# Attention's products of the 16 meta keys with V: one float32r product of 96 stacked rows in place of float32 products of 16 rows

## The chip, the cores and the metric

One core of one Trainium2 chip runs the whole program. The metric is the device time of one execution in microseconds (us); the median of a few executions counts. A difference of 0.2% (about 5.4 us) is what a measurement of this kernel can tell from no change.

## The reference, cut to what matters

The program computes two transformer blocks on a sequence of 1024 tokens. The change touches the first one only, which has two layers, 1024 features and 16 learned meta tokens ahead of the sequence, so 1040 positions. In each layer attention is done twice, once by four "differential" heads and once by eight "forgetting" heads:

```python
s = einsum('bhmqd,bhmkd->bhmqk', qb, k) * scale       # differential: two maps per head
p = softmax(where(visible, s, -inf), axis=-1)
a = p[:, :, 0] - lam * p[:, :, 1]
out = einsum('bhqk,bhkd->bhqd', a, v)                 # v is 128 wide

s = einsum('bhqd,bhkd->bhqk', qb, k) * scale + cq[..., None] - cum_logf[:, :, None, :]
p = softmax(where(visible, s, -inf), axis=-1)         # forgetting
out = einsum('bhqk,bhkd->bhqd', p, v)                 # v is 64 wide
```

The rows that matter here are the keys k of the last product: 1024 keys of the sequence, in 8 tiles of 128, and the 16 meta keys, which every query sees.

## The kernel before, in words

**Groups, blocks and maps.** The heads are worked in eight groups g. Groups 0 to 3 are one differential head each (its two softmax maps are merged on VectorE before the product with V, so there is one product map, 128 columns of V wide). Groups 4 to 7 are two forgetting heads each (two product maps m, 64 columns wide each, that write to the two halves of PSUM's partitions). Queries are worked in blocks of two tiles of 128, `BLOCKS` = (6,7), (4,5), (2,3), (0,1), and in layer 0 a last block (8,) of the 16 meta queries alone; layer 1 leaves that one out, since its output is not needed.

**Steps of a block.** `step_scores` computes the scores (float32r products on 64 rows) into PSUM, `step_max`, `step_exp` and `step_norm` make the softmax in tile `P` (part of `top`). Then `step_tr` transposes P with TensorE, two key tiles at a time, into one of three PSUM banks (`FEW` = 5, 6, 7); the first part (n = 0) is the 16 meta keys alone, "tile 8". `step_pt` copies each part to `PT` (also part of `top`), on ScalarE (L1894) or VectorE (L2657, and L2659/L2660 for the last, half empty part), as the planner chose. When all parts are copied, `step_av` multiplies with V: for each key tile one float32 product per map. Tile 8 comes first: `V[0:16]` against `PT[0:16]`, 16 rows, 256 query columns. A tile that only the second query tile sees has 128 columns. `step_av_out` (L1856) takes the result out of PSUM.

**How V gets there.** `step_turn_v` transposes the projected V in three pieces (quads); quad 2 is the 16 meta rows, and `step_v_out` on ScalarE copies them into `V[0:16, ..., 8, :]` (L1869).

**Precision.** A product of float32 tiles appears in the trace as two weight loads and two MATMUL records. A product of float32r tiles has one of each. Where the kernel uses float32r it splits each operand into a high part (a float32r copy) and a low part (the rest), and makes three products: high x high, high x low, low x high. The projections (`step_unit`, `mm3`) do this: `AH`, `AL` are the activations, `WH`, `WL` the weights.

**What sets the order.** `attention_order` plans each layer before the program is built: `Clocks` keeps a model of when TensorE, ScalarE, VectorE, GpSimd and the DMA queue are free, and puts the next TensorE step from four lists (scores; transposes and products with V; projection units of the next groups; small ones), and the evacuations by `PRIORITY` and due time. The cost of a step stands in `cost` and `side_of`: a product step costs 216 ns for the last tile, 432 for each other, 610 for tile 8, plus 150. Projection units fill the time between attention steps, one at a time in one of the three `FEW` banks. Each engine then runs its list in that order.

All helper calls record the same source line: L1078 is every product, L1087 every transpose, so steps are told apart by the tiles they read. `PS<-top,V` are the products with V, `PS<-AH,WH` and so on the projection units, `PS<-ident,top` the transposes of P, `PS<-KH,QH` and `PS<-maskr,eyer` the scores.

## Time and profile before

| what | value |
|---|---|
| median of 3 runs | 2723.8 us (2722.2 to 2727.41) |
| the profiled execution's own time | 2731.44 us |
| its span, first to last instruction | 2729.6 us |
| mean granted TensorE clock | 0.988 |
| TensorE busy (MATMUL) | 2649.7 us, 97% |
| VectorE / ScalarE / GpSimd busy | 1637.5 / 1201.0 / 466.2 us |
| layer 0's attention, layer 1's attention | about 100 to 720 us, about 840 to 1500 us |

The profiled execution is 1.8 us longer than its span and 7.6 us longer than the median. A row of the timeline gives the start and the length of an instruction (or of a run of like ones); on TensorE the lengths overlap, since a product's record begins when it is taken up and ends when its last result is out, so cost is read from start to start. PE is TensorE's products, PEld its weight loads, DVE VectorE, ACT ScalarE. Shapes read as rows*columns of the stationary operand, then rows x columns of the moving one.

### The profile page before, as it was taken

What the parts mean: (1) busy time and instruction counts of PE and PEld (TensorE: products, weight loads), DVE (VectorE), ACT (ScalarE), POOL (GpSimd) and SP (SyncE); (2) the same over time, 40 slices, a digit from 0 to 9 for tenths busy, and PEclk for the clock granted to TensorE, in tenths of its full rate; (3) what the DMA queues carried; (4) which work ended last, traced back from release to release, by engine and by line L of the source; (5) the groups of instructions that cost most, each with busy time, mean ns of one, the idle gap of its engine ahead of it and who ended that gap; (6) DMA issues with size and microseconds to landing.
All of it is one profiled execution on the core that took longest, in us unless ns stands there. A gap on an engine that the chain in (4) does not pass through costs nothing.

```text
span 2729.6 us, 43070 instructions
## 1 busy us (share of the span) xinstructions
PE 2649.7 (97%) x16632; PEld 2278.5 (83%) x16632; DVE 1637.5 (60%) x2944; ACT 1201.0 (44%) x2372; POOL 466.2 (17%) x674
## 2 busy tenths in 40 slices
PE   6999999999999999999999999999998999999999
PEld 6888888888899888878777997888897788887887
DVE  5766664444535666554446366555437877778767
ACT  6444444333424444443334462223335655555444
POOL 2211232310001222452000124000013101011000
PEclk9999999999999999999999899999998999999999
DMA  4121377761312212897202423113232344444443
GB/s 150 57 67 64 120 191 198 202 158 44 142 58 74 74 64 74 245 233 182 82 24 78 129 72 114 47 47 100 93 92 95 116 127 121 124 126 153 177 154 135
DMA packets 219225, 314.21 MB, mean 115 GB/s; under 512 B 15478, under 2 KB 157494, under 8 KB 219022
## 3 DMA queue, kind: packets, MB, share of 16 engines
q0 software_dynamic: 50304, 151.30, 19.2%
q1 hardware_dynamic: 168720, 160.16, 18.6%
q8 instruction: 134, 2.20, 0.3%
q14 instruction: 67, 0.55, 0.1%
HBM read 267.26 MB, written 111.22 MB: 139 GB/s over the span
## 4 chain that ended last, share of the span: by engine, by line
PE 84%; DVE 6%; ACT 3%; issue 2%; DMA 2%; POOL 2%; SPq 0%; DVEq 0%; ACTq 0%; POOLq 0%
PE PS L1078 79%; PE PS L1087 5%; DMA T<-TMP 2%; DVE WL L2451 1%; DVE AL L2494 1%; POOL TMP L3427 1%; DVE ST L2623 0%; DMA R<-s_adap 0%; DVE TMP L2606 0%; POOL T L3424 0%; DVE T L2599 0%; ACT top L1881 0%; ACT TMP L1830 0%; DVE top L2636 0%; ACT TMP L1720 0%
## 5 line engine op out<-in xcount | busy, mean ns | idle before, releaser
L1078 PE MATMUL PS<-AH,WH 128*128 128x344 f32 (+2 forms) x2160 | 805.0, 373 | 23.7 <-DVE AL L2494 9.4
L1078 PE MATMUL PS<-AL,WH 128*128 128x344 f32 (+2 forms) x2160 | 756.8, 350 | 0.0
L1078 PE MATMUL PS<-AH,WL 128*128 128x344 f32 (+2 forms) x2160 | 756.3, 350 | 0.0
L1078 PEld LDWEIGHTS PS<-AH,WH 128*128 128x128 f32 x2160 | 408.8, 189 | 83.5 <-issue 21.0
L1078 PEld LDWEIGHTS PS<-AH,WL 128*128 128x128 f32 x2160 | 408.5, 189 | 36.0
L1078 PEld LDWEIGHTS PS<-AL,WH 128*128 128x128 f32 x2160 | 409.8, 190 | 32.1 <-issue 1.0
L1078 PE MATMUL PS<-WH,AH 128*128 128x256 f32 (+1 forms) x972 | 309.4, 318 | 3.7 <-DVE WL L2451 3.7
L1078 PE MATMUL PS<-WL,AH 128*128 128x256 f32 (+1 forms) x972 | 308.6, 317 | 0.0
L1078 PE MATMUL PS<-WH,AL 128*128 128x256 f32 (+1 forms) x972 | 308.6, 317 | 0.0
L2623 DVE TENSOR_REDUCE ST<-PS 128x1 f32<-128x784 f32 (+8 forms) x272 | 187.9, 732 | 143.0 <-PE PS L1078 142.5
L2451 DVE TENSOR_TENSOR WL<-W,WH 128x1024 fp32r<-128x1024 f32 x157 | 192.6, 1229 | 125.6 <-ACT WH L1708 125.5
L1881 ACT ACTIVATE top<-PS,ST 128x784 f32<-128x784 f32 (+8 forms) x272 | 194.9, 722 | 111.7 <-DVE ST L2623 87.7
L1708 ACT ACTIVATE WH<-W 128x1024 fp32r<-128x1024 f32 x157 | 165.3, 1055 | 119.9 <-PE PS L1078 105.4
L1078 PEld LDWEIGHTS PS<-WH,AH 128*128 128x128 f32 x972 | 185.5, 191 | 18.6 <-issue 4.5
L1078 PEld LDWEIGHTS PS<-WH,AL 128*128 128x128 f32 x972 | 185.6, 191 | 12.1
L1078 PEld LDWEIGHTS PS<-WL,AH 128*128 128x128 f32 x972 | 185.5, 191 | 12.0
L1078 PE MATMUL PS<-top,V 128*64 128x256 f32 (+6 forms) x1176 | 183.3, 373 | 2.9 <-DVE top L2660 2.4
L1087 PE MATMUL PS<-ident,top 128*128 128x128 f32 (+2 forms) x1132 | 172.5, 276 | 5.9 <-DVE AL L2494 3.3
L1078 PEld LDWEIGHTS PS<-top,V 128*64 128x64 f32 (+3 forms) x1176 | 119.6, 154 | 67.3 <-issue 39.3
L1087 PEld LDWEIGHTS PS<-ident,top 128*128 128x128 f32 (+2 forms) x1132 | 127.7, 133 | 32.6 <-ACT top L1894 3.8
L1894 ACT ACTIVATE top<-PS 128x512 f32<-128x512 f32 (+1 forms) x167 | 82.7, 500 | 147.3 <-PE PS L1087 146.0
L3147 DVE TENSOR_TENSOR WL<-W,WH 128x512 fp32r<-128x512 f32 x116 | 90.3, 781 | 75.1 <-ACT WH L2230 75.1
(406 smaller groups left out, 4419.5 us busy)
## 6 DMA issues: line engine op xcount, KB each, us to landing
W<-in_k_w_in SPq DMA_DIRECT2D x66, 512.0 KB, 4.2
s_wt<-in_w_up POOLq DMA_DIRECT2D x96, 352.0 KB, 6.3
W<-in_w_ada SPq DMA_DIRECT2D x48, 512.0 KB, 5.2
s_wd<-in_w_down POOLq DMA_DIRECT2D x66, 256.0 KB, 6.3
W<-s_wt SPq DMA_DIRECT2D x64, 256.0 KB, 3.5
W<-in_w_in SPq DMA_DIRECT2D x28, 512.0 KB, 3.8
W<-in_w_up SPq DMA_DIRECT2D x52, 256.0 KB, 3.3
W<-in_w_out SPq DMA_DIRECT2D x24, 512.0 KB, 3.5
```

Of the source, the lines that this page charges most:

```text
L1078: return e.matmul(out, lhsT, rhs, start=start, stop=stop, skip_group_check=True)
L1087: return e.transpose(out, in_, ident[0:k, 0:k])
L1708: e.activation(high(v), W32[:, s, :], ACT.Copy).then_inc(*w_hi.mark(v))
L1881: e.activation(P[0:rows, P_SLOT[u], 0:W], PSf[0:rows, o:o + W], ACT.Exp, bias=st[:, 0:1], accum_out=st[:, 1:2]).then_inc(*exped.mark(u))
L1894: e.activation(o, i, ACT.Copy).then_inc(*pt_act.mark(key))
L2451: e.tensor_tensor(low(v), W32[:, slot32(v), :], f(high(v)), ALU.subtract).then_inc(*w_lo.mark(v))
L2494: e.scalar_tensor_tensor(lo, bank(b)[:, o:o + n], COLS[:, 8 * l + k:8 * l + k + 1], f(hi), ALU.mult, ALU.subtract).then_inc(*fill_lo.mark( ...
L2623: e.tensor_reduce(ST[0:rows, ST_SLOT[u], 0:1], PSf[0:rows, o:o + W], AX.X, ALU.max, negate=True).then_inc(*row_max.mark(u))
L3147: e.tensor_tensor(lo, up_source(i), f(hi), ALU.subtract).then_inc(*w_lo.mark(("up", i)))
L3427: e.tensor_tensor(TMP[:, cc:cc + nn], TMP[:, cc:cc + nn], cosT[:, cc:cc + nn], ALU.mult).then_inc(*rope_cos.mark(key))
```

## The change

The meta keys' product becomes float32r on 96 rows. Rows 0 to 31 of the stacked P hold the high part of the transposed probabilities, rows 32 to 63 the low part, rows 64 to 95 the high part again; the stacked V holds high, high, low. One product so sums the three terms. Only 16 of each 32 rows are real; the transposes now turn 32 columns, and the surplus rows of V are multiplied by 0 (a new constant column, `OF_META`).

- New tiles `V3a`, `V3b` (stacked V, one for each parity of the group) and `P3` (stacked P, two slots); `V` and `PT` lose their ninth tile.
- For two-map groups each map's product is 128 columns wide, the other map's 64 columns of V3 being zero, so both maps add into the whole bank, one after the other.
- `step_pt` makes two copies instead of one for part 0, on the same engine. A new VectorE step `pt_lo` makes the low part and only then frees the bank. `step_v_out` for quad 2 makes two copies (four for two-map groups), and a new VectorE step `v_lo` makes V's low part.
- `step_av` waits for `v_lo` and `pt_lo` beside the other parts; the product of tile 8 stays the first.
- The planner's costs follow (tile 8 costs 210 instead of 610; the meta block 200 instead of 400; part 0's copies 600 or 750 ns, `pt_lo` 440, `v_lo` 500), so the whole order of both layers is planned anew.

```diff
-            V = own("V", [128, 2, 9, 128])[:, :, :, :]
+            V, V3a = own("V", [128, 2, 8, 128])[:, :, :, :], own("V3a", [128, 256], F32R)
...
-            top = own("top", [128, 4 * L + 2 * 9 * 256])
+            top = own("top", [128, 4 * L + 2 * 8 * 256])
+            P3 = own("P3", [128, 2, 256], F32R)
+            V3 = [V3a[:, :], own("V3b", [128, 256], F32R)[:, :]]
...
                     if blk == (8,):
-                        return 400
+                        return 200
...
-                    return sum(216 if t == blk[1] else 432 if t < 8 else 610 for t in tiles) + 150
+                    return sum(216 if t == blk[1] else 432 if t < 8 else 210 for t in tiles) + 150
...
-                b = turn_bank(("pt",) + key, (pt_act if PT_SIDE[key] == "act" else pt_dve, key))
+                b = turn_bank(("pt",) + key, (pt_lo if n == 0 else pt_act if PT_SIDE[key] == "act" else pt_dve, key))
...
+                        if t == 8:
+                            x = tr(e, bank(b)[0:32, 128 * jj:128 * jj + rows], P[0:rows, P_SLOT[l, g, j, m], 0:32])
...
-                e.wait_ge(*v_turned.at((l, g, 2)))
+                e.wait_ge(*v_turned.at((l, g, 1)))
+                e.wait_ge(*v_lo.at(("v", l, g)))
                 for m in maps(g):
-                    for n in range(len(parts(l, g, bi))):
+                    e.wait_ge(*pt_lo.at((l, g, bi, m, 0)))
+                    for n in range(1, len(parts(l, g, bi))):
...
-                        kr = NM if t == 8 else 128
-                        qa = 128 if (not meta and t == blk[1]) else 0
-                        x = mm(e, bank(b)[r0:r0 + rn, qa:nq], V[0:kr, vs, t, r0:r0 + rn], PT[0:kr, PT_SLOT[l, g, bi, m], t, qa:nq],
-                               i == 0, i == len(tiles) - 1)
+                        if t == 8:
+                            x = mm(e, bank(b)[:, 0:nq], V3[vs][0:96, 128 * m:128 * m + 128], P3[0:96, slot_, 0:nq], m == 0, meta and m == maps(g)[-1])
+                        else:
+                            qa = 128 if t == blk[1] else 0
+                            x = mm(e, bank(b)[r0:r0 + rn, qa:nq], V[:, vs, t, r0:r0 + rn], PT[:, slot_, t, qa:nq], False, i == len(tiles) - 1)
...
+                    if n == 0:
+                        e.activation(P3[64:96, PT_SLOT[l, g, bi, m], 0:i.shape[1]], i, ACT.Copy)
                     e.activation(o, i, ACT.Copy).then_inc(*pt_act.mark(key))
...
+                        if n == 0:
+                            e.tensor_copy(P3[64:96, pt, 0:i.shape[1]], i)
                         e.tensor_copy(o, i).then_inc(*pt_dve.mark(key))
...
+                def step_pt_lo(g, bi, m, n):
+                    key = (l, g, bi, m, n)
+                    pt, nq, b = PT_SLOT[l, g, bi, m], NM if BLOCKS[l][bi] == (8,) else 256, banks.place.get(("pt",) + key, 0)
+                    side_ = pt_act if PT_SIDE[key] == "act" else pt_dve
+                    e.wait_ge(*side_.at(key))
+                    e.tensor_tensor(P3[32:64, pt, 0:nq], bank(b)[0:32, 0:nq], f(P3[0:32, pt, 0:nq]), ALU.subtract).then_inc(*pt_lo.mark(key))
+
+                def step_v_lo(g):
+                    vs, b = g % 2, banks.place.get(("vt", l, g, 2), 0)
+                    e.wait_ge(*v_turned.at((l, g, 2)))
+                    if g in (4, 5):
+                        e.tensor_tensor(V3[vs][0:96, 64:192], ident[0:96, :], ident[0:96, :], ALU.subtract)
+                    for (o, i), (hi, _) in zip(cols3(g, vs, 64, 96, b), cols3(g, vs, 0, 32, b)):
+                        x = e.scalar_tensor_tensor(o, i, OF_META[0:32, :], f(hi), ALU.mult, ALU.subtract)
+                    x.then_inc(*v_lo.mark(("v", l, g)))
```

## Rows read from the trace of the kernel before

**Rows 1.** The page's part 1: TensorE's busy time, share of the span, instructions

```profile
PE 2649.7 (97%) x16632; PEld 2278.5 (83%) x16632; DVE 1637.5 (60%) x2944; ACT 1201.0 (44%) x2372; POOL 466.2 (17%) x674
```

**Rows 2.** The page's part 4: the chain that ended last, by engine

```profile
PE 84%; DVE 6%; ACT 3%; issue 2%; DMA 2%; POOL 2%; SPq 0%; DVEq 0%; ACTq 0%; POOLq 0%
```

**Rows 3.** Busy times in both layers' attention; last columns: PEclk, DMA share, GB/s

```profile
100.00:720.00 620.00, 610.53 (x4489) 527.76 (x4486) 353.29 (x785) 261.53 (x586) 130.31 (x192) 1.00 0.43 121
840.00:1500.00 660.00, 647.34 (x4418) 538.22 (x4417) 377.46 (x761) 284.04 (x578) 149.02 (x221) 0.99 0.40 112
```

**Rows 4.** PE's longest waits, 100 to 720 and 840 to 1500: total, times, longest

```profile
PE PS L1078 <- ACT FIN L1901: 3.3, 2, 1.7
...
PE PS L1078 <- ACT top L1881: 4.6, 7, 2.0
```

**Rows 5.** PE's timeline around two product steps of one-map groups: start, length

```profile
114.88 4.13 PE L1078 MATMUL PS<-top,V 16*128 16x256 f32 x18
118.77 0.40 PE L1078 MATMUL PS<-AH,WH 128*128 128x344 f32 x1
...
138.03 0.32 PE L1078 MATMUL PS<-AH,WL 128*128 128x344 f32 x1
138.28 3.27 PE L1078 MATMUL PS<-top,V 16*128 16x256 f32 x14
141.30 0.40 PE L1078 MATMUL PS<-AH,WH 128*128 128x344 f32 x1
141.54 0.31 PE L1078 MATMUL PS<-AL,WH 128*128 128x344 f32 x1
```

**Rows 6.** The weight loads of the second of these steps, idle time in brackets

```profile
138.27 0.29 PEld L1078 LDWEIGHTS PS<-top,V 16*128 16x128 f32 x2 [0.22 <-issue]
138.90 2.46 PEld L1078 LDWEIGHTS PS<-top,V 128*128 128x128 f32 x12 [0.33 <-issue]
141.27 0.19 PEld L1078 LDWEIGHTS PS<-AH,WH 128*128 128x128 f32 x1
```

**Rows 7.** PE's timeline around a product step of a two-map group

```profile
430.22 0.31 PE L1078 MATMUL PS<-AH,WL 128*128 128x344 f32 x1
430.47 4.04 PE L1078 MATMUL PS<-top,V 16*64 16x256 f32 x36
...
434.69 0.32 PE L1078 MATMUL PS<-AL,WH 128*128 128x344 f32 x1
```

**Rows 8.** The weight loads of that step

```profile
430.46 0.19 PEld L1078 LDWEIGHTS PS<-top,V 16*64 16x64 f32 x4 [0.21 <-issue]
431.04 3.22 PEld L1078 LDWEIGHTS PS<-top,V 128*64 128x64 f32 x32 [0.38 <-issue]
434.43 0.19 PEld L1078 LDWEIGHTS PS<-AH,WH 128*128 128x128 f32 x1 [0.17 <-issue]
```

**Rows 9.** PE's timeline in the output projection: float32r products of 256 columns

```profile
1499.92 0.28 PE L1078 MATMUL PS<-WH,AL 128*128 128x256 f32 x1
1500.04 0.28 PE L1078 MATMUL PS<-WH,AH 128*128 128x256 f32 x1
```

**Rows 10.** PE's timeline around a product step of the 16 meta queries

```profile
185.25 0.32 PE L1078 MATMUL PS<-AH,WL 128*128 128x344 f32 x1
...
185.82 0.39 PE L1087 MATMUL PS<-ident,top 128*16 128x128 f32 x2
```

**Rows 11.** Groups by shape, first 1500 us: evacuations; busy us, mean ns

```profile
L1894 ACT ACTIVATE top<-PS 16x256 f32<-16x256 f32 x59 | 21.9, 371 | 58.5 <-PE PS L1087 57.9
...
L2657 DVE COPY top<-PS 16x256 f32<-16x256 f32 x37 | 15.2, 410 | 9.7 <-PE PS L1087 9.2
...
L2590 DVE SCALAR_TENSOR_TENSOR KL<-PS,KH 128x344 fp32r<-128x344 f32 x16 | 8.1, 508 | 9.9 <-ACT KH L1834 9.9
```

**Rows 12.** The end of layer 0's attention, timeline

```profile
716.28 0.42 DVE L2659 COPY top<-PS 128x256 f32<-128x256 f32 x1 [0.38 <-PE PS L1087]
...
717.04 1.45 PE L1078 MATMUL PS<-top,V 16*64 16x256 f32 x12 [0.81 <-DVE top L2660]
```

More of the change, by code:

```diff
@@ L497, in build @@
         class Clocks:
-            PRIORITY = {"leave": 0, "leave_lo": 0, "pt": 0, "max": 1, "av_out": 0, "v_out": 0, "rope": 0, "rope_sin": 0, "ada_out": 1, "fin_ms": 1, "exp": 1, "norm": 1,
+            PRIORITY = {"leave": 0, "leave_lo": 0, "pt": 0, "max": 1, "av_out": 0, "v_out": 0, "pt_lo": 0, "v_lo": 0, "rope": 0, "rope_sin": 0, "ada_out": 1, "fin_ms": 1, "exp": 1, "norm": 1,
                         "forget": 2, "rope_add": 2, "rope_end": 2, "rope_lo": 2, "fin1": 2, "fin3": 2, "gate": 2, "split": 3, "split_lo": 3, "root": 3,
@@ L650, in place @@
                     out.append(("pt",) + st[1:])
+                    if n == 0:
+                        out.append(("pt_lo",) + st[1:])
                 elif what == "av":
@@ L663, in place @@
                         if st[2] == 2:
+                            out.append(("v_lo", st[1]))
                             self.tmp = [end] * 3
@@ L702, in side_of @@
                         return ready, 740
+                    if n == 0:
+                        return ready, (600, 750)
                     return ready, (170 + 1.02 * wide, 250 + 0.68 * wide)
+                if what == "pt_lo":
+                    return at["hi", st[1:]], 440
+                if what == "v_lo":
+                    return at["hi", "v", st[1]], 500
                 if what == "av_out":
@@ L788, in put_side @@
                     self.side[st[1:]] = engine
+                    if st[4] == 0:
+                        at["hi", st[1:]] = seen
+                    else:
+                        self.leave(("tr",) + st[1:], back)
+                        at[st] = back
+                elif what == "pt_lo":
                     self.leave(("tr",) + st[1:], back)
-                    at[st] = back
+                    at[("pt",) + st[1:]] = back
                 elif what == "av_out":
@@ L808, in put_side @@
                         at["qk", st[1], st[2]] = back
+                elif what == "v_out" and st[2] == 2:
+                    at["hi", "v", st[1]] = seen
                 elif what == "v_out":
@@ L811, in put_side @@
                     at[("v",) + st[1:]] = back
+                elif what == "v_lo":
+                    self.leave(("turn_v", st[1], 2), back)
+                    at["v", st[1], 2] = back
                 elif what == "ada_out":
@@ L1063, in build @@
         g_out, g_in = o_in, tile_in
+        pt_lo, v_lo = conv_v, g_v
         down_mm, down_act, down_dve, end_sq, end_v, out_done = (count("down_mm"), count("down_act"), count("down_dve"), count("end_sq"),
@@ L1187, in step_turn_v @@
                 key = (l, g, quad)
-                b = turn_bank(("vt",) + key, (v_turned, key))
+                b = turn_bank(("vt",) + key, (v_turned, key) if quad < 2 else (v_lo, ("v", l, g)))
                 e.wait_ge(*proj_out.at((l, g, "v", 2)))
-                for i, t in enumerate(range(4 * quad, min(4 * quad + 4, 9))):
-                    cc, n = (NM + 128 * t, 128) if t < 8 else (0, NM)
-                    m = tr(e, bank(b)[0:n, 128 * i:128 * i + 128], TMP[:, cc:cc + n])
+                if quad == 2:
+                    m = tr(e, bank(b)[0:32, 0:128], TMP[:, 0:32])
+                else:
+                    for i, t in enumerate(range(4 * quad, 4 * quad + 4)):
+                        m = tr(e, bank(b)[:, 128 * i:128 * i + 128], TMP[:, NM + 128 * t:NM + 128 * t + 128])
                 m.then_inc(*vt_mm.mark(key))
@@ L1260, in step_tr @@
                         e.wait_ge(*normed.at((l, g, j, 1 if g < 4 else m)))
-                kr = NM if part[0] == 8 else 128
                 for i, t in enumerate(part):
                     for jj, j in enumerate(blk):
-                        if t < 8 and t > j:
-                            continue
                         rows = NM if j == 8 else 128
-                        ka = 0 if t == 8 else NM + 128 * t
-                        x = tr(e, bank(b)[0:kr, 256 * i + 128 * jj:256 * i + 128 * jj + rows], P[0:rows, P_SLOT[l, g, j, m], ka:ka + kr])
+                        if t == 8:
+                            x = tr(e, bank(b)[0:32, 128 * jj:128 * jj + rows], P[0:rows, P_SLOT[l, g, j, m], 0:32])
+                        elif t <= j:
+                            ka = NM + 128 * t
+                            x = tr(e, bank(b)[:, 256 * i + 128 * jj:256 * i + 128 * jj + 128], P[:, P_SLOT[l, g, j, m], ka:ka + 128])
                 x.then_inc(*pt_mm.mark(key))
@@ L1868, in step_v_out @@
                     else:
-                        e.activation(V[0:NM, vs, 8, :], bank(b)[0:NM, 0:128], ACT.Copy).then_inc(*v_turned.mark((l, g, quad)))
+                        for o, i in cols3(g, vs, 0, 32, b):
+                            e.activation(o, i, ACT.Copy, scale=OF_META[0:32, :])
+                        for o, i in cols3(g, vs, 32, 64, b):
+                            x = e.activation(o, i, ACT.Copy, scale=OF_META[0:32, :])
+                        x.then_inc(*v_turned.mark((l, g, quad)))
                 def step_exp(g, j):
@@ L2425, in scalar, with cols3 @@
             ffn()
+        def cols3(g, vs, r0, r1, b):
+            if g < 4:
+                return [(V3[vs][r0:r1, 0:128], bank(b)[0:32, 0:128])]
+            return [(V3[vs][r0:r1, 192 * m:192 * m + 64], bank(b)[0:32, 64 * m:64 * m + 64]) for m in range(2)]
         def pt_evac(l, g, bi, part, pt, b):
@@ L2431, in pt_evac @@
                 nq = NM if blk == (8,) else 256
-                return PT[0:NM, pt, 8, 0:nq], bank(b)[0:NM, 0:nq]
+                return P3[0:32, pt, 0:nq], bank(b)[0:32, 0:nq]
             return PT[:, pt, part[0]:part[0] + 2, :].rearrange("p a b -> p (a b)"), bank(b)
@@ L3758, in layout @@
         cols[r:128:32, 20 + r % 2] = 1.0
+    for r in range(NM):
+        cols[r:128:32, 22] = 1.0
     a["k_cols"] = cols
```

9 lines of the change are left out of this document (7 added, 2 removed).

## The prediction, made before the changed kernel ran

> **What bounds the kernel now.** I read the busy shares first: TensorE is busy 97% of the span, VectorE 60%, ScalarE 44% [rows 1]. The chain that ended last is 84% TensorE [rows 2]. The change touches only the two layers' attention, so I asked for the busy times there: TensorE 610.5 of 620 us and 647.3 of 660 us, idle 9.5 and 12.7 us in all; VectorE 353 and 377 us (57%), ScalarE 262 and 284 us (43%) [rows 3]. The longest of TensorE's waits sums to 3.3 us in one layer and 4.6 us in the other [rows 4]. So TensorE bounds both stretches, and projection units fill the gaps between attention's steps. A microsecond taken from its products should shorten the span by nearly one, as long as the others keep up.
>
> **TensorE, one-map groups.** A product step of 18 records takes 3.89 us from its start to the next unit's, one of 14 records 3.02 us [rows 5]: four records more for 0.87 us, 0.216 us a record of 256 columns, 0.432 us a float32 product, half of that for 128 columns. From the last unit record before the second step (138.03) to the second one after it (141.54) are 3.51 us. Two units of 0.16 us belong to that, so the step costs 3.19 us. Its six tile products take 5 x 0.432 + 0.216 = 2.37 us. **Tile 8 so costs 0.82 us**, not 0.43. The other 0.39 us stand in the weight loads: the 16-row load begins only after 0.22 us of idle loader, the first 128-row load after 0.33 us, but the load of the unit behind the step has no idle time before it [rows 6]. A load of the same shape as the running product is hidden under it. Where the shape changes, it waits for the stream's end and is then exposed itself: some 0.195 us at each of the two changes.
>
> After the change tile 8 is one float32r product of 256 columns: 1500.04 - 1499.92 = 0.12 us [rows 9]. Its 96 rows are my first unknown; no row shows 96. If the array takes them as it takes 128, both changes of shape vanish and the step saves 0.82 - 0.12 = 0.70 us. If 96 counts as a shape of its own, both stay, and it saves 0.82 - 0.12 - 0.39 = 0.31 us. I take the first: 96 rows need more than half of the array, and a product of 128 rows is the nearest. There are 32 such steps (four groups, four blocks, two layers). 11 of them follow a score or a small product in the trace, where the entry stays exposed (0.51 us saved); 21 follow a unit. Sum: 21 x 0.70 + 11 x 0.51 = 20.3 us.
>
> **Two-map groups.** The two maps' products run side by side on 64 columns each: 36 records in the time of 18 [rows 7]. From 430.22 to 434.69 are 4.47 us, less two units 4.15, less 7 x 0.432 + 0.216 = 3.24 leaves 0.91 us. Of this 0.20 us is the way out to a unit: 0.17 us of idle loader, then an exposed load [rows 8]. That way out is not touched. Tile 8 so costs 0.71 us for the pair: 0.43 and two changes of shape of 0.14 each (the loads are half as wide). After: two products, one after the other because each covers all 128 columns, 2 x 0.12 = 0.24 us; the entry from a unit has no change of shape, but the change from 128 columns to 64 behind it stays, 0.14. Saved 0.71 - 0.24 - 0.14 = 0.33 us. This change of shape is where a rule speaks against the edit. The Trainium skill, TensorEngine Tiling (Array Packing), Key Properties, says that a change of tiling mode, not merely of the tile, drains TensorE; by that rule the trace's 0.14 us stay, and without a drain 32 x 0.14 = 4.5 us more would be saved. With 96 as its own shape the entry costs 0.195 and only 0.14 us are saved. Of 32 steps 27 follow a unit, 5 a score or a transpose (0.14 us): 27 x 0.33 + 5 x 0.14 = 9.6 us.
>
> **The eight steps of the meta queries**, layer 0 only. Now 185.82 - 185.25 - 0.16 = 0.41 us [rows 10]; one load of 128 columns in its place is about 0.12. I take 0.25 us each, between nothing and 0.41: 2 us.
>
> **Transposes.** The part of the meta keys turns 32 columns for 16, against the same 128 moving columns. Only their weight loads grow by 16 columns. If all of that were exposed, at the 0.195 us that an exposed 128-column load and its wait cost, it would be 0.195 / 8 on 108 parts, 2.6 us; I take nothing, since loads that follow a product of the same shape are hidden [rows 6].
>
> TensorE's sum: 20.3 + 9.6 + 2 = **32 us**; 15 us if 96 is its own shape (32 x 0.31 + 32 x 0.14 + 0.5).
>
> **VectorE and ScalarE.** There are 96 parts of meta keys of 256 columns and 12 of 16. Now each costs one copy, 371 ns on ScalarE (59) or 410 ns on VectorE (37) [rows 11]. The second copy adds 59 x 0.37 = 22 us and 37 x 0.41 = 15 us. `pt_lo` reads PSUM and a tile: the nearest row is 508 ns for 344 columns [rows 11], bounds for 256 columns are 0.41 (a copy's row) and 0.51; I take 0.42: 40 us, and 2 for the small ones. V's stacked rows, 16 groups of a few short pieces at 0.2 to 0.3: 7 us on VectorE, 7 on ScalarE. VectorE gains 64 us on 731, ScalarE 29 on 546, over 1250 us: 64% and 46% busy. That lies under TensorE's units while there are any. If the cover is gone, a meta part costs 0.41 + 0.42 + 0.06 us of signals more than now before its product may start.
>
> **Where it is not covered: the ends of the layers.** At the end of layer 0 no unit is left, and TensorE waits 0.81 us for VectorE's copies [rows 12]. Here the bank's two extra operations stand ahead of those copies in VectorE's queue. The last two blocks of layer 0 and of layer 1 pay; between nothing (ScalarE takes the copies) and 4 x 0.9 x 2 maps = 7 us. I take 3 us. In the middle, VectorE's wait for ScalarE's copy in `pt_lo` holds up the maxima and normalizations queued behind it, for which `step_exp` and `step_tr` wait, and a bank of the three is held some 0.9 us longer. Bounds: nothing, and as much idle time again as both stretches have now, 22 us [rows 3]. I take 3 us, as VectorE is a third idle even then.
>
> **Sum.** 32 - 3 - 3 = 26 us off the profiled execution's 2731.4 us. This one is 7.6 us above the median, 2723.8 us, so the median becomes **2698 us**. Own range of this case: 2690 (all 32 us and a luckier plan) to 2706.
>
> **Rivals.**
> 1. *96 rows is a shape of its own, or one of the drains stays.* TensorE then gains 15 us, less 6: 9 us, 2715 us. For it: all rows with a row count other than 128 pay (16 here) [rows 6]. Against: 16 rows use an eighth of the array, 96 cannot be packed beside anything. The Trainium skill's page named above lists row tilings of 128, 64 and 32 rows alone under Tiling Modes; it has none of 96, so by it this rival does not happen, and no row here shows it. Chance 0.13.
> 2. *The gain is half eaten by the side engines*: VectorE gets 64 us more and TensorE 32 us less cover; stalls of 16 us instead of 6 leave 16 us, 2708 us. For it: the three banks, and 4.6 us of waits on ScalarE's exponentials already [rows 4]. Against: a total idle time of 22 us in 1280 [rows 3]. Chance 0.09.
> 3. *The low part becomes the wait that sets the pace.* Every product step starts with tile 8, so it waits for `pt_lo` first. If `pt_lo` stands so late in VectorE's queue that TensorE idles 0.5 us or more in each of the 64 steps, the whole 32 us are gone; from there it is slower. At 0.8 us, what it waits at the layer's end today [rows 12], it loses 64 x 0.8 - 32 = 19 us: 2743 us. Against: part 0 is transposed first, and up to four more parts follow it, so it has more than a microsecond of lead in the long blocks. Only block (0,1) has a single part behind it. Chance 0.04.
> 4. *It doesn't do what it says*: the float32r product runs no faster than the float32 one. Then only the drains go and two-map groups get slower (two products for a pair side by side): 32 x 0.39 - 32 x (0.43 - 0.14) = 3 us less, 6 more lost: 2727 us. The float32r units speak against it [rows 9]. Chance 0.02.
>
> The likeliest case keeps 0.72. The range goes from 2690 to 2715, up to rival 1's figure; about 0.17 lie outside. Faster by over 0.2% (5.4 us, about what a measurement can tell) are the first case and rivals 1 and 2 but for their edges: 0.91. Within it 0.05, slower 0.04.
>
> **What the changed profile would show.** Tile 8's loads should read 96*128, and in one-map steps neither they nor the first 128*128 load behind them should have idle time before them (against 0.22 and 0.33 us [rows 6]); the step of the 14 records should shrink to 13 and by 0.7 us. In two-map steps an idle loader should remain ahead of the first 128*64 load. TensorE's busy time in the two stretches should fall by about 30 us, VectorE's rise by 64. Idle TensorE should grow by 6 us, mostly at the ends. I am wrong if the 96-row load stands after an idle gap (rival 1), if waits on `P3` or banks sum to over 15 us (rival 2), or if they come in every step (rival 3).

## The result, and the profile after

The changed kernel takes 2748.75 us (median of 4 runs, 2747.44 to 2750.02) against 2724.65 us for the kernel before beside it: a ratio of 1.0088, interval 1.0071 to 1.0106. It is 24 us slower where 26 us faster were forecast, and outside the range. The profiled execution took 2747.65 us, its span is 2745.9 us.

The page of the changed kernel, its busy times and its chain:

```profile
PE 2631.7 (96%) x16524; PEld 2283.4 (83%) x16524; DVE 1702.8 (62%) x3132; ACT 1227.4 (45%) x2460; POOL 466.5 (17%) x674
...
PE 77%; DVE 8%; issue 7%; ACT 4%; DMA 2%; POOL 2%; ACTq 0%; DVEq 0%; SPq 0%; POOLq 0%
```

TensorE has 18 us less to do than in [rows 1]; VectorE has 65 us more and ScalarE 26 us more, close to what was foreseen. But TensorE's share of the chain fell from 84% [rows 2] to 77%. Busy times in the two stretches of [rows 3] (last columns PEclk, DMA share, GB/s):

```profile
100.00:720.00 620.00, 595.38 (x4395) 527.81 (x4392) 371.07 (x853) 273.85 (x631) 129.96 (x191) 0.99 0.43 121
840.00:1500.00 660.00, 636.97 (x4334) 541.69 (x4334) 403.58 (x828) 284.29 (x590) 150.80 (x222) 0.99 0.40 113
```

TensorE's busy time fell by 25.5 us, 30 were foreseen (VectorE's rose by 44 us in these two stretches; the rest of its 65 us lies outside them). But the work did not go forward: both stretches hold 178 records fewer than before (4395 + 4334 against 4489 + 4418), some 100 of them the change's own, and the rest were done later. The time saved went idle.

**The product steps did shrink.** TensorE's products and weight loads around the one-map step of [rows 5 and 6], now with 13 records in place of 14:

```profile
139.24 0.33 PE L1102 MATMUL PS<-AH,WL 128*128 128x344 f32 x1
139.41 0.28 PE L1102 MATMUL PS<-P,V3a 96*128 96x256 f32 x1
139.53 2.54 PE L1102 MATMUL PS<-top,V 128*128 128x256 f32 x12
141.83 0.40 PE L1102 MATMUL PS<-AH,WH 128*128 128x344 f32 x1
142.07 0.32 PE L1102 MATMUL PS<-AL,WH 128*128 128x344 f32 x1
```

```profile
139.25 0.19 PEld L1102 LDWEIGHTS PS<-P,V3a 96*128 96x128 f32 x1
139.41 2.47 PEld L1102 LDWEIGHTS PS<-top,V 128*128 128x128 f32 x12
141.80 0.19 PEld L1102 LDWEIGHTS PS<-AH,WH 128*128 128x128 f32 x1
```

No idle loader is left before either load, and from the last unit record before the step to the second one after it are 142.07 - 139.24 = 2.83 us, against 3.51: 0.68 us saved, 0.70 were foreseen. So 96 rows run as 128 do. The two-map step of [rows 7 and 8] has now:

```profile
430.29 0.30 PEld L1102 LDWEIGHTS PS<-P,V3a 96*128 96x128 f32 x2 [0.32 <-DVE GT L2628]
430.73 3.22 PEld L1102 LDWEIGHTS PS<-top,V 128*64 128x64 f32 x32
434.12 0.19 PEld L1102 LDWEIGHTS PS<-AH,WH 128*128 128x128 f32 x1 [0.17 <-issue]
```

Tile 8 takes 430.73 - 430.29 = 0.44 us of the loader for the pair, against 431.04 - 430.46 = 0.58 [rows 8]; the step is 3.83 us long instead of 3.97. This step stands behind a wait. In the 24 two-map steps that follow a projection unit directly the pair takes 0.34 us (median from the first record to the next tile's), before 0.58. Added up from start to start over all product steps, idle gaps left out, they fell from 173.5 to 149.4 us, and the records just ahead of them, which bear the entry, from 18.1 to 14.3 us: 28 us saved. Of these, 19.5 us lie in the one-map steps, 7.0 in the two-map steps and 1.2 in those of the meta queries.

In the two-map step 0.14 us lie between the end of the second load, at 430.59, and the next one; in 30 of the 32 two-map steps this gap is 0.13 or 0.14 us. The Trainium skill, TensorEngine Tiling (Array Packing), Key Properties, has a change of tiling mode drain TensorE; the trace agrees with it.

**Where it went.** Added up in the same way, TensorE's idle gaps from 60 us to the output projection in layer 0, and from 850 us in layer 1, were 13.3 + 10.4 = 23.7 us before and are 32.6 + 28.2 = 60.7 us now. TensorE's waits in the whole program (total, times, longest):

```profile
PE PS L1102 <- ACT top L1915: 12.0, 20, 2.0
PE PS L1102 <- DVE P L2711: 10.5, 9, 2.3
...
PE PS L1111 <- DVE P L2711: 5.2, 9, 1.4
...
PE PS L1111 <- ACT OTt L1886: 4.1, 2, 3.1
PE PS L1102 <- ACT OTt L1886: 3.9, 3, 3.0
PE PS L1102 <- DVE V3a L2719: 3.6, 3, 1.3
```

L2711 is `pt_lo`: products wait for it 10.5 us, transposes for the bank that it holds 5.2 us. L1915 is the exponentials, for which TensorE waited 6.4 us in the whole program before:

```profile
PE PS L1078 <- ACT top L1881: 6.4, 10, 2.0
```

L1886 is `step_av_out`; before, TensorE waited 0.4 us in all for it. The cause of the new wait can be read in three views, ScalarE's and TensorE's timelines, and the busy times from 430 us:

```profile
428.81 0.46 ACT L1853 ACTIVATE GT<-PS 128x344 f32<-128x344 f32 x1 [0.63 <-PE PS L1102]
442.23 0.38 ACT L1886 ACTIVATE OTt<-PS 128x256 f32<-128x256 f32 x1 [12.97 <-DMA s_os<-OTt]
```

```profile
442.67 0.41 PE L1111 MATMUL PS<-ident,top 128*32 128x128 f32 x2 [3.06 <-ACT OTt L1886]
445.30 1.12 PE L1111 MATMUL PS<-ident,top 128*128 128x128 f32 x4 [2.22 <-DVE GT L2628]
```

```profile
430.00:440.00 10.00, 9.41 (x70) 7.71 (x67) 1.49 (x3) 0.00 (x0) 1.94 (x3) 1.00 1.05 238
440.00:450.00 10.00, 5.11 (x23) 4.67 (x23) 2.89 (x5) 2.87 (x5) 0.00 (x0) 0.66 0.06 26
```

The next group's result may not be written to `OTt` until the gate's store `s_os<-OTt` of the group before has landed. GpSimd issues that store at 429.98 us, behind a burst of eight background transfers (last two rows of the burst, and the store):

```profile
428.94 1.60 POOL L3455 DMA_DIRECT2D s_wt<-s_wt  x1
429.46 1.91 POOL L3458 DMA_DIRECT2D s_wt<-s_wt  x1
429.98 1.95 POOL L3491 DMA_DIRECT2D s_os<-OTt  x1
```

It lands 12.2 us later. ScalarE does nothing from 430 to 440 us, then TensorE runs dry twice. From 442.9 to 449.7 us, so from the end of the first gap on, its granted clock is the lower one: 0.66 on average from 440 to 450 us, its units starting every 0.29 us at the lower of the two levels (1.2 GHz) in place of 0.16 us at 2.4. From 100 us to the end of layer 1's attention, the stretches at the lower level add up to 37.5 us, before to 13.7 us. TensorE was idle in 5.2 us of the 37.5 and in 0.3 us of the 13.7. Half of what is left is lost: 16 us now, 7 us before, so 9 us more.

The sum over the two layers is then 28 us saved, 37 us more idle, 9 us more by the clock, and some 3 us in the transposes of 32 columns: 21 us longer. The traces agree: the output projection of layer 1 starts at 1520.0 us instead of 1499.6, 20.4 us later. This is not the whole of the 24 us between the medians. The two profiled executions are only 16 us apart, since the one of before was 7 us above its median, and behind that point the changed kernel's execution is 4 us the faster one, though nothing was changed there. So the parts of the sum are good to a few microseconds, not to one.

### The profile page after: what moved, and what is told of

Same layout as the page of the kernel before. It is cut to its first block, busy times and chain, and to the rows that moved or that the text cites. A ratio compares the mean times of both kernels' runs of the same rounds, so it can differ in the third digit from the quotient of the medians.

```text
span 2745.9 us, 43150 instructions
## 1 busy us (share of the span) xinstructions
PE 2631.7 (96%) x16524; PEld 2283.4 (83%) x16524; DVE 1702.8 (62%) x3132; ACT 1227.4 (45%) x2460; POOL 466.5 (17%) x674
## 4 chain that ended last, share of the span: by engine, by line
PE 77%; DVE 8%; issue 7%; ACT 4%; DMA 2%; POOL 2%; ACTq 0%; DVEq 0%; SPq 0%; POOLq 0%
PE PS L1102 72%; PE PS L1111 4%; DMA T<-TMP 1%; DMA s_os<-OTt 1%; DVE ST L2665 1%; ACT top L1915 1%; DVE AL L2536 1%; DVE WL L2493 1%; DVE P L2711 0%; POOL TMP L3487 0%; DVE top L2681 0%; DVE P L2701 0%; ACT R L1983 0%; DVE top L2701 0%; ACT TMP L1860 0%
## 5 line engine op out<-in xcount | busy, mean ns | idle before, releaser
L1915 ACT ACTIVATE top<-PS,ST 128x784 f32<-128x784 f32 (+8 forms) x272 | 194.5, 721 | 93.0 <-DVE ST L2665 68.6
L1102 PE MATMUL PS<-top,V 128*64 128x256 f32 (+1 forms) x960 | 139.8, 368 | 0.0
L1102 PEld LDWEIGHTS PS<-top,V 128*64 128x64 f32 (+1 forms) x960 | 102.8, 157 | 30.9 <-issue 2.3
L3469 POOL DMA_DIRECT2D s_adap<-AST x48 | 29.1, 606 | 532.5 <-DVE AST L2573 515.9
```

Of the source, the lines that this page charges most:

```text
L1102: return e.matmul(out, lhsT, rhs, start=start, stop=stop, skip_group_check=True)
L1915: e.activation(P[0:rows, P_SLOT[u], 0:W], PSf[0:rows, o:o + W], ACT.Exp, bias=st[:, 0:1], accum_out=st[:, 1:2]).then_inc(*exped.mark(u))
L3469: e.dma_start(adap[i % 2][:, 256 * (i // 2):256 * (i // 2) + 256], AST[:, i % 2, :]).then_inc(*ada_out[i % 2].landed(i))
```

## Experiments

Idle is TensorE's, added up as above in each profile. The ratio compares the means of the runs with the runs of the kernel before that were taken beside them. Their medians lay between 2724.65 and 2727.25 us, so kernels are best compared by the ratio, and 0.001 of it is 2.7 us. In a row of idle times 2 us mean nothing: the gap of 1.5 to 2.3 us with which layer 1 begins falls ahead of 850 us in some kernels and behind it in others.

| kernel | operations | order planned by | us | ratio to before (interval) | idle us |
|---|---|---|---|---|---|
| before | old | before | 2724.65 | 1 | 23.7 |
| after | new | after | 2748.75 | 1.0088 (1.0071 to 1.0106) | 60.7 |
| oldops_newplan | old | after | 2747.69 | 1.0082 (1.0064 to 1.0100) | 40.8 |
| newops_oldplan | new | before | 2765.14 | 1.0141 (1.0120 to 1.0162) | 70.8 |
| nolo | new, no `pt_lo` | after | 2735.43 | 1.0033 (1.0022 to 1.0045) | 51.8 |
| nolo_oldplan | new, no `pt_lo` | before | 2715.90 | 0.9965 (0.9953 to 0.9976) | 38.5 |
| oldops_loplan | old | low parts alone | 2777.72 | 1.0188 (1.0170 to 1.0207) | 62.2 |
| newops_loplan | new | low parts alone | 2778.70 | 1.0187 (1.0170 to 1.0203) | 81.6 |
| store_first | new, sums later | after | 2740.99 | 1.0051 (1.0037 to 1.0064) | 53.6 |
| late | new, tile 8 last | after | 2744.05 | 1.0066 (1.0052 to 1.0080) | 60.3 |
| both | both of these | after | 2737.88 | 1.0047 (1.0034 to 1.0060) | 53.2 |
| onecopy | new, one copy less | after | 2739.12 | 1.0047 (1.0031 to 1.0063) | 56.1 |
| truecost | new | after, copies at 860 | 2751.41 | 1.0093 (1.0079 to 1.0106) | 67.5 |
| oldplan_late | new, tile 8 last | before | 2759.76 | 1.0120 (1.0104 to 1.0136) | 71.0 |
| before620 | old | before, tile 8 at 620 | 2724.17 | 0.9997 (0.9986 to 1.0007) | 23.2 |
| k128 | float32, 128 rows | before | 2714.44 | 0.9959 (0.9946 to 0.9972) | 26.5 |
| k128_store | same, sums later | before | 2713.22 | 0.9957 (0.9944 to 0.9969) | 29.1 |
| k128_432 | same | before, tile 8 at 432 | 2720.43 | 0.9978 (0.9968 to 0.9987) | 31.8 |

**Operations against order.** oldops_newplan is the kernel before with the changed planner (`Clocks` and `attention_order`); the new steps that it plans are not issued.

> The products, copies and waits of the kernel before, but every engine's list in the order that the changed planner makes (its costs, with pt_lo and v_lo planned and then not issued). Theory A, the new order carries the loss (background transfers, banks and queues meet otherwise): 15 to 35 us slower than before, 2740 to 2760 us. Theory B, the low part's own operations and waits carry it: within 6 us of before, 2719 to 2731 us. In between means both.

newops_oldplan is the changed kernel with the planner of before, each low part put right behind its copy:

```diff
+        def with_low(steps):
+            out = []
+            for st in steps:
+                out.append(st)
+                if st[0] == "pt" and st[4] == 0:
+                    out.append(("pt_lo",) + st[1:])
+                if st[0] == "v_out" and st[2] == 2:
+                    out.append(("v_lo", st[1]))
+            return out
```

> The changed operations, but every engine's list in the order of the planner of before, pt_lo put directly behind its copy and v_lo behind V's copy. Theory A: the saving on TensorE (24 us from start to start in the two traces) shows, less a few us of stalls: 2702 to 2714 us. Theory B: the stalls come again: 2735 to 2755 us.

The old operations lose 22 us (1.0082) in the new order: theory A held, and the order alone is as slow as the whole change. But the new operations lose more in the old one, 38 us, which is slower than either theory allowed. There, VectorE's queue stands at `pt_lo` for ScalarE's copy (VectorE's waits, in that kernel and in the changed one):

```profile
DVE P L2703 <- ACT P L1922: 65.5, 41, 6.0
```

```profile
DVE P L2711 <- ACT P L1930: 8.4, 24, 0.6
```

The changed planner brings these 65.5 us down to 8.4: it makes the room that the low part needs, and pays with an order that is worse in other places. For the new operations as a whole the new order is the better one, by 14 us (1.0141 less 1.0088). A part of the 38 us may belong to the placing in this run, which puts each low part directly behind its copy, also where the copy is ScalarE's; a low part that stands later in VectorE's queue was not run in the old order.

The two runs split the result. In the new order the new operations take 2 us more than the old ones (1.0088 less 1.0082), though they save 28 us on TensorE: what they bring with them costs 30 us there, the transposes' 3 us among it. So the 24 us are 22 us of order and 30 us of the operations' own stalls, less 28 us saved. In the old order these stalls cost 66 us (38 and the 28 saved).

**Without the low part.** nolo is the changed kernel in its own order without `pt_lo`:

```diff
-                    e.wait_ge(*pt_lo.at((l, g, bi, m, 0)))
-                    for n in range(1, len(parts(l, g, bi))):
+                    for n in range(len(parts(l, g, bi))):
...
                 def step_pt_lo(g, bi, m, n):
-                    key = (l, g, bi, m, n)
...
+                    return
```

> The changed kernel in its own order, but pt_lo is not issued: rows 32 to 63 of P3 stay zero, the bank is free after the copy and the product waits for the copy only. It leaves out the term P low x V high. All other operations and their order are the same. Theory A: the order's stalls stay, 2738 to 2748 us. Theory B: the 16 us of TensorE's waits on pt_lo and what hangs on them go, 2715 to 2730 us.

nolo took 2735 us, between the two outcomes: 15 us come back (1.0088 less 1.0033), and part of the stalls stays. nolo_oldplan is the same in the order of before.

> The new operations in the order of the kernel before, without the low part of P's meta rows (that part of the product is left out: P low with V high), so with the second copy and V's low part alone as extra work. The same without the low part in the changed order took 2735 us. If the changed order itself costs some 20 us whatever the operations (as it does for the old ones), this one runs at 2735 - 20 = 2715 us or under; TensorE's 24 us saved less the second copies' stalls would then at last be seen below the kernel before. If the changed order is only bad for operations that don't have the low part, it is no faster than 2735 us. With the low part in this order 2765 us were measured; so the difference to it is what the low part costs where the order makes no room for it: 30 to 50 us by the first theory.

The first theory held: 2715.9 us, 9.5 us faster than before, and 19.5 us faster than in the new order. So the new order costs 22 us with the old operations and 18 us without the low part (1.0033 less 0.9965), and the low part costs 15 us in the new order (1.0088 less 1.0033) and 48 us in the old one (1.0141 less 0.9965). Even without either, of the 28 us saved on TensorE 18 are gone, to the second copies, V's low part and the longer chain: 38.5 us idle against 23.7.

**A third order.** oldops_loplan and newops_loplan take the changed planner with the old costs of TensorE's steps:

```diff
-                        return 200
+                        return 400
...
-                    return sum(216 if t == blk[1] else 432 if t < 8 else 210 for t in tiles) + 150
+                    return sum(216 if t == blk[1] else 432 if t < 8 else 610 for t in tiles) + 150
```

> The kernel before with its own operations, in the order that the changed planner gives when it plans the low parts but keeps the old costs of TensorE's product steps (610 for the meta tile, 400 for the meta queries). It splits the 23 us by which the old operations lose in the changed order (2748 us). If planning with TensorE's cheaper steps spoils the order (the planner thinks that VectorE and ScalarE are late and the background goes to other places), this one runs at about 2727 us. If the low parts' 440 and 600 ns in the side engines' queues spoil it, about 2747 us. If any change of order does about as much harm, between them, with other stores behind other transfers.

> All new operations, in the order of a planner that knows the low parts but keeps the old costs of TensorE's product steps. The old operations took 2778 us in this order, 30 us more than in that of the full planner. If a bad order is bad for any operations, this one takes about 2749 + 30 = 2779 us; if it was bad only because that planner expected slower side engines than the old operations have, it comes to about 2750 us.

Both take 51 us more than before, to within a microsecond of each other, so here too the stalls of the new operations eat the 28 us that they save. For the first run this was none of the three outcomes that I gave; for the second, the first outcome came. It is not a rule that an order is as bad for any operations: in the order of before the new ones lose 38 us. TensorE's longest wait of all in oldops_loplan, and in oldops_newplan, is for the exponentials, 6.4 us in the kernel before:

```profile
PE PS L1098 <- ACT top L1901: 26.1, 21, 3.7
```

```profile
PE PS L1098 <- ACT top L1901: 13.1, 18, 2.0
```

These operations are untouched by the change, and their wait goes with the order, whatever the operations: 6.4 to 9.0 us in the six kernels whose TensorE, ScalarE and VectorE follow the order of before, 11.3 to 13.4 in the seven that follow that of the changed kernel, 26 in both of this third order. That they come late since the scores, maxima and exponentials stand elsewhere in the queues is argued, not shown. The opposite planner, with the new TensorE costs alone, was not run.

**The stores.** In store_first GpSimd's background sums go behind a gate's store that follows directly:

```diff
                         if at_ > turns:
-                            weight_sums(next(sums))
+                            held = [x[0] for x in STEPS[l][at_ + 1:] if x[0] in ("ada_out", "rope", "gate", "reload")][:1] == ["gate"]
+                            if not held:
+                                weight_sums(next(sums))
```

> The changed kernel with one thing moved: on GpSimd's queue a group of background transfers (the weight sums, eight or more of them) that stands directly ahead of the store of a finished group is issued behind that store. In the new order three stores of layer 0 stand behind such a group (at 430, 503 and 591 us), in the order of before none stands behind more than four. If this collision carries the order's loss: ScalarE's longest wait for a store falls from 13 us to under 5 and the kernel is 8 to 15 us faster than the changed one, 2733 to 2741 us. If it only explains the one gap at 440 us: 2742 to 2746 us. If nothing: 2747 to 2751 us.

It takes 2741 us: some 8 to 10 us of the loss. ScalarE's longest wait for a store falls from 13.0 to 3.5 us. This wait belongs to the order and not to the operations, since the old ones have it too (ScalarE's waits in oldops_newplan and in the kernel before):

```profile
ACT OTt L1876 <- DMA s_os<-OTt: 24.5, 5, 14.0
```

```profile
ACT OTt L1856 <- DMA s_os<-OTt: 11.9, 6, 3.1
```

In store_first the stretch that had been empty is full again:

```profile
430.00:440.00 10.00, 10.00 (x73) 9.17 (x69) 3.48 (x7) 3.44 (x6) 0.76 (x1) 1.00 1.02 213
440.00:450.00 10.00, 9.78 (x80) 8.09 (x80) 6.24 (x19) 4.20 (x12) 6.12 (x9) 1.00 0.75 249
```

**Where the wait stands.** late takes tile 8 last in each product step, and waits for `v_lo` and `pt_lo` only there:

```diff
+                tiles = tiles[1:] + tiles[:1]
                 for i, t in enumerate(tiles):
+                    if t == 8:
+                        e.wait_ge(*v_lo.at(("v", l, g)))
+                        for m in maps(g):
+                            e.wait_ge(*pt_lo.at((l, g, bi, m, 0)))
```

> The changed kernel in its own order, but the product of the meta keys stands last in its step and the waits on pt_lo and v_lo stand directly before it. If the low part costs by making the product wait (10.5 us of waits on P before products): 2738 to 2744 us. If it costs by holding one of three banks and by VectorE's time: unchanged, 2746 to 2751 us.

It gains some 5 us, but its interval (1.0052 to 1.0080) overlaps that of the changed kernel. The product comes later and still waits: products wait 8.8 us for `pt_lo`, without this edit 10.5, and the transposes' 5.2 us of waits for the bank stay (5.1). So the run moves the wait and hardly removes it. both joins it with store_first.

> Both partial remedies in the changed kernel: tile 8's product last with its waits (late, measured 2744 us) and GpSimd's background sums behind the gate's store (store_first, 2741 us), against 2749 us unmended. If the two losses are separate they add up: 2749 - 8 - 5 = 2736 us, 1.003 to 1.004 of before. If they are one loss seen twice (the late product only bridges the time in which ScalarE stands at the store) it stays at about 2741 us. If the idle time amplifies itself through the halved clock, the two together give more than their sum, under 2732 us.

2737.9 us lies between 2736 and 2741, with intervals that overlap those of store_first: the second remedy adds at most a few microseconds to the first, and the run doesn't settle how many. oldplan_late is late in the order of before.

> All new operations in the order of the kernel before (2765 us), with tile 8's product moved from first to last in each step and its waits with it. If those 2765 us come from the waits of the product steps on VectorE's P3 (10.2 us of waits there, and the clock that falls in them), late products take 10 to 20 us off: 2750 us. If they come from the bank held longer and from VectorE's own wait for ScalarE's copy (65.5 us over 41 waits in that order), which the maxima and normalizations queue behind, it stays at 2762 us or more.

It took 2760 us, between the two outcomes, and its interval overlaps that of newops_oldplan. Here too the waits did not go: products wait 11.1 us for `pt_lo` (10.4 in newops_oldplan), and VectorE waits 64.6 us for ScalarE's copy (65.5). So the run doesn't tell what these waits cost. That the low part as a whole costs 48 us in this order is shown by nolo_oldplan; how this divides between the products' waits, the held banks and VectorE's queue is not.

**Length or load.** onecopy leaves out the second copy (rows 64 to 95 of `P3` stay zero).

```diff
-                        if n == 0:
-                            e.tensor_copy(P3[64:96, pt, 0:i.shape[1]], i)
```

> The changed kernel, same order, without the second copy of P's high part (rows 64 to 95 of the stacked tile stay zero, so the product of P's high with V's low part is left out). 37 copies of about 0.43 us leave VectorE and 59 of 0.37 leave ScalarE. If it is the length of the chain between a transposed part and its product (copy, copy, low part) that makes the stalls, 0.4 us of 1.3 go from each of 108 chains and the time falls about as far as without the low part's subtraction (2735 us): 2737 us. If only VectorE's queue counts, 15 us less work there gives a third of what leaving out the low part gave (13.5 us for 47 us of VectorE's work): 2745 us. If the order alone counts: 2749 us, nothing.

11 us come back (1.0088 to 1.0047), nearly as much as without `pt_lo` (15 us), though VectorE loses 16 us of work here and 41 us there. TensorE's waits for `pt_lo` fall from 15.7 to 11.4 us. This speaks for the first theory, the length of the chain from a transposed part to its product, and against VectorE's load alone. It doesn't part the chain from ScalarE, which loses 21 us of work here and none in nolo, nor from the bank, which is free one copy earlier.

**Truer costs.** truecost plans the two copies closer to what they take on VectorE (415 and 413 ns, and what lies between); before620 plans the kernel before with 10 ns more for tile 8.

```diff
-                        return ready, (600, 750)
+                        return ready, (860, 750)
```

```diff
-                    return sum(216 if t == blk[1] else 432 if t < 8 else 610 for t in tiles) + 150
+                    return sum(216 if t == blk[1] else 432 if t < 8 else 620 for t in tiles) + 150
```

> The changed kernel, with the planner's cost of part 0's two copies on VectorE at the 860 ns that the trace shows (two starts 0.43 us apart and the next 0.45 us later) instead of 600. If stalls come from a plan that thinks VectorE faster than it is: 5 to 12 us faster than the changed kernel, 2736 to 2744 us. If not: another order with stalls like these, 2744 to 2755 us.

> The kernel before, where the planner's cost of tile 8 is 620 ns instead of 610. No operation changes, only the order. If the order of before is one that any small move of a cost spoils (a lottery in which before holds a good ticket): 5 us or more away from before, most likely slower, 2730 to 2745 us. If orders from nearly equal costs are equally good, and the new one is bad for its own reasons: within 4 us of before.

Neither moved the time beyond its interval. But before620 hardly moves the order either: of the 3835 steps in the planner's lists of both layers only some 40 stand elsewhere than in the kernel before, against some 300 between truecost and the changed kernel, and some 1700 between the changed kernel and the one before. So these two runs show that small moves do no harm. They don't show that a plan made wholly anew is no throw of dice.

**The change of shape alone.** k128 is the kernel before with tile 8's float32 product over 128 rows, the 112 that are no meta keys multiplied by zero:

```diff
-                        kr = NM if t == 8 else 128
+                        kr = 128
...
-                        e.activation(V[0:NM, vs, 8, :], bank(b)[0:NM, 0:128], ACT.Copy).then_inc(*v_turned.mark((l, g, quad)))
+                        e.activation(V[:, vs, 8, :], bank(b)[:, 0:128], ACT.Copy, scale=COLS[:, 22:23]).then_inc(*v_turned.mark((l, g, quad)))
```

> The kernel before with one thing changed: the float32 product of the meta keys runs over 128 rows instead of 16, V's 112 other rows being zero. No operation is added, the order is that of before. If a changed shape costs what the prediction took from the rows (0.195 us at both ends of tile 8 in one-map groups after a unit, 0.14 us at its end in two-map groups): 32 x 0.195 + 21 x 0.195 + 32 x 0.14 = 15 us faster, 2706 to 2714 us. If the 0.39 us belong to float32 products of few rows as such: the same as before or up to 5 us slower from moving things.

It beats both kernels, 11 us faster than before where 15 were expected, with no new wait and no new operation but one clearing of a tile at the start. The product steps with the records ahead of them fell by 16 us (from 191.5 to 175.3, the changed kernel's to 163.7). Its weight loads at the same one-map step, 14 records with no idle time between the unit's load and theirs:

```profile
137.30 0.19 PEld L1078 LDWEIGHTS PS<-AH,WL 128*128 128x128 f32 x1
137.46 2.94 PEld L1078 LDWEIGHTS PS<-top,V 128*128 128x128 f32 x14
140.31 0.19 PEld L1078 LDWEIGHTS PS<-AH,WH 128*128 128x128 f32 x1
```

k128_store adds store_first's edit, k128_432 tells the planner 432 for tile 8.

> The best version so far (the kernel before, float32 product of the meta keys over 128 rows, 2714.4 us) with the background sums of GpSimd issued behind the gate's store where one follows directly. In the kernel before one store alone stands behind 4 such transfers and waits at most 3.1 us. If a store behind transfers costs only by its length over what covers it, there is nothing to gain: 2714 us. If every microsecond of it counts, up to 3 us: 2711 us. If the delayed transfers come late for the next layer, it is slower: 2717 us.

> The best version (float32 product of the meta keys over 128 rows, 2713 to 2714 us) with its true cost of 432 ns told to the planner in place of 610. If a truer cost gives a better order, 2708 to 2712 us. If every new order is a draw around the tuned one's time, and the tuned one is among the good ones, 2715 to 2735 us.

The stores had nothing to give there (0.9957 against 0.9959); the longest wait behind one was 3.1 us before and 4.6 us in k128. The truer cost moved some 1000 steps and made the kernel 5 to 6 us slower (0.9978 against 0.9959), the second of its two outcomes.

## Why the prediction was wrong, step by step

- **TensorE's steps: right.** 32 us foreseen, 28 measured. One-map steps saved 19.5 us of 20.3; the step shown saves 0.68 us where 0.70 stood. Two-map steps saved 7.0 of 9.6: behind a unit they save about 0.30 us instead of 0.33, as tile 8's pair takes 0.34 us (0.24 + 0.14 foreseen) but the record ahead of it shrank by 0.07, not by 0.14. The meta queries saved 1.2 of 2. Rival 1 did not happen.
- **Transposes: a small miss.** The 32-column loads take 97 ns against 89, and the steps cost some 3 us more, near the bound of 2.6 that was given and not taken.
- **VectorE and ScalarE: sizes right, conclusion wrong. This is the step that failed.** `pt_lo` took 414 ns (0.42 foreseen), VectorE gained 65 us, ScalarE 26. The prediction then said of the stalls in the middle of the layers "I take 3 us, as VectorE is a third idle even then", and with 3 us for the ends all stalls came to 6 us. They cost 30 us in the new order (after against oldops_newplan, with the 28 us saved) and 66 us in the old one. The bound of 22 us was too low as well. The busy share says nothing of a queue worked in order with a wait at its head, as the 65.5 us of newops_oldplan show; and onecopy speaks for the chain's length rather than VectorE's load.
- **The ends: right in size.** At the end of layer 0 TensorE waits 2.31 and 1.10 us for `pt_lo`, before 0.81 [rows 12] and 0.4 for others.
- **No term for the order.** "The whole order of both layers is planned anew" stood ahead of the prediction, and its steps priced a new plan only as a chance of luck, at the lower end of the range. This is the second missing term: 22 us with the old operations and 18 without the low part. Its size and even its sign hang on what runs in the order, as the whole of the new operations loses 14 us less in the new one. Some 8 to 10 us, measured with the new operations, are stores that stand behind eight transfers in GpSimd's queue. The prediction followed the queues of TensorE, VectorE and ScalarE, but neither GpSimd's nor its transfers.
- **No term for the clock.** Before, with 24 us of idle time, TensorE ran 13.7 us at the lower level; with 61 us of idle time it ran 37.5 us there, and lost 9 us more by it. These 9 us are within the two terms above, not beside them.
- **Rival 3** came near in time (2743 us, at 0.04) by luck: its mechanism is only a part of what happened. `pt_lo` is waited for 18 times for 15.7 us in all, not in each of 64 steps, and its sum has no order in it. Rival 2 had the mechanism, stalls of the side engines, but 16 us where 30 came, and nothing for the order.

What stays open: why the new order is worse beyond the stores. The exponentials are late in it, but no single decision of the planner was found that makes the loss. Nor is it excluded that the order of before is simply a good one, to which any wide new plan loses: the three orders that move 1000 steps or more all did, by 5, 22 and 51 us.

## What to carry to other kernels

When an edit changes the costs of a planner, or steps that it places, the old operations in the new order are a run of their own, to be made first: here this alone cost 22 us, nearly as much as the whole change. An engine that is a third idle is no cover for operations put on the chain between a transpose and its product, when its queue is worked in order and there are three banks. And before a product is made cheaper in its arithmetic, look whether it is only its shape that costs: multiplying 16 keys and 112 rows of zeros gave 11 us, with no new instruction in the attention.

## What the runs showed of the hardware

- A float32 product of 16 rows between products of 128 left the loader idle for 0.22 us ahead of its load and 0.33 us behind it [rows 6]. A float32r product of 96 rows left it idle at neither end (the loader's rows at 139.25 and 139.41), and neither did a float32 product of 128 rows (k128, at 137.46).
- Between the load of a 96-row, 128-column product and the next of 64 columns lay 0.13 or 0.14 us in 30 of 32 steps.
- A store issued behind eight transfers of 352 KB on GpSimd's queue landed after 12.2 us; moving the transfers behind it gave back 8 to 10 us of the whole.
- A gap of 3.06 us that ended at 442.67 us was followed by the lower clock level from 442.9 to 449.7 us. A second gap, of 2.22 us, lies within this stretch, and behind it units start every 0.29 us, from 446.51 to 447.68 us. Time at the lower level, added up as in the account of the result, goes up with idle time among the kernels of the table: from 3.4 us (k128_store, 29.1 us idle) over 17.1 (nolo_oldplan, 38.5) and 37.5 (the changed kernel, 60.7) to 50.6 (newops_loplan, 81.6). It does so not strictly: truecost, 67.5 us idle, has 28.9. So idle time of the engine that sets the pace is in part paid for again.
